# Halving the first expert selection of each layer, and moving every fourth row's dot product from VectorE to GpSimd and ScalarE

## The chip, the core and the metric

The program runs on one core of a Trainium2 chip. A core has TensorE (PE in the profile: matrix products), VectorE (DVE), ScalarE (ACT), GpSimd (POOL) and SyncE (SP, which here only issues transfers), each with an instruction queue of its own that it works through in order, and 16 DMA engines that move data between the chip's memory (HBM) and the on-chip buffer SBUF. Engines wait for each other through semaphores. The metric is the device time of one execution in microseconds (us); all arithmetic is in float32.

## The reference, cut to what matters

256 tokens of width 1024 pass through two layers (attention, then a feed-forward "PEER" block), and after them through a third block with recurrent mixers and a mixture of experts, which the change doesn't touch. The PEER block, for a chunk `xc` of 128 tokens:

```python
q = (xc @ wq).reshape(128, 8, 2, 128)                 # 8 heads, 2 sides
sc = jnp.einsum('chpd,hpnd->chpn', q, sub_keys)       # 128 key scores for each head and side
s1, i1 = lax.top_k(sc[:, :, 0], 16)
s2, i2 = lax.top_k(sc[:, :, 1], 16)
cand = s1[..., :, None] + s2[..., None, :]            # 256 candidates for each head
cidx = i1[..., :, None] * 128 + i2[..., None, :]
top_s, pos = lax.top_k(cand, 16)
eidx = take_along_axis(cidx, pos)                     # 16 of 16384 experts for each head
g = softmax(top_s)
a = gelu(einsum('chkd,cd->chk', u[eidx], xc))         # dot product with the expert's u
out = einsum('chk,chkd->cd', g * a, v[eidx])          # weighted sum of the experts' v
```

So each token picks 8 x 16 = 128 experts for each layer. For each the row `u` (1024 numbers) is multiplied with the token and summed up, and the row `v` is weighted and added.

## The kernel before, in words

Tokens lie on the 128 partitions. Each layer `l` has a **first chunk** (attention of tokens 0 to 127, then the peer queries and key scores), written out engine by engine, and a **peer stage** of 256 **rows**: row `n` is the n-th chosen expert of every token of a chunk (rows 0 to 127 of tokens 0 to 127, the others of tokens 128 to 255). In one row:

- GpSimd issues the gather (`gather`, line 2705): one indirect DMA brings to each partition the 2048 numbers (u and v) of its token's expert, 1 MB in all, into one of 8 landing places (`GATHERS = 8`; place `n % 8`). It waits until the numbers of the experts are there (`idx`), and for row n - 8 to have been used by TensorE.
- VectorE makes the dot product (`dots`, line 1551): one instruction that multiplies and sums, 128 x 1024, both inputs in SBUF, followed by a short one that reads out the accumulator.
- ScalarE (`weigh`, line 125) takes gelu of it, scales it by the softmax weight and writes a diagonal matrix of 64 columns.
- TensorE multiplies this with the row's v: 8 matmuls (`weighted_sum`, line 155; 64x64 tiles in the rows of the profile), and adds up in PSUM over 128 rows.

The experts are chosen by VectorE in **selections** (`route(q)`), four for a layer, each of four heads, for 64 rows (q = 0: rows 0 to 63). A selection is cut into 24 **pieces** (`yield`): 8 of `topk` over 128 scores, one that adds up candidates (128 x 1024), 4 of `topk` over 256 candidates, one of small steps, 6 over a one-hot table `OH` (128 x 1024: compare, multiply, reduce, for two sides), and the last steps with `idx_u`. `route(0)` runs whole before the first row. `route(q + 1)` has one piece on every second row of the 64 before (k = 2, 4, ... 48), `weights` (sum and reciprocal for the softmax) comes at k = 54, `exp_of` on ScalarE at k = 50.

Beside the rows each engine runs a **background**: rows 3, 5, ... 59 carry the attention of tokens 128 to 255 and their queries and key scores (`second_chunk`), later rows the third block's context (features in layer 0, states in layer 1) and in layer 0 the next layer's first projections. Each engine advances its background by one step at a fixed row (`beside`; GpSimd five rows later than its gathers count). So the order on each engine is written out by hand, and one engine's wait for another's background step holds back its rows as well. SyncE loads the weights (2 MB blocks) when their places in the `ring` come free.

In layer 0 the first chunk also has twelve `modulation` products with weights of their own, and the first gather waits until the tenth of them has left the place that it lands in (`("used", "w_mod", 10, 1)`). In layer 1 there is nothing of that; the gathers of places 2 to 7 wait for the queries' weights to be used.

## Time and profile before

| | us |
|---|---|
| median of three runs | 2847.54 |
| the runs | 2843.93 to 2849.05 |
| the profiled execution | 2847.81 |
| its span in the profile | 2846.0 |
| TensorE busy | 2144.6 (75%) |
| VectorE busy | 1585.1 (56%) |
| ScalarE busy | 832.7 (29%) |
| GpSimd busy | 749.6 (26%) |
| peer stage of layer 0, first gather to last sum | 191.4 to 948.4 |
| peer stage of layer 1 | 1096.6 to about 1825 |

How to read it: the busy shares are means over stages with different limits. Rows arrive fastest every 2.5 us in both peer stages, and the times at which a row is gathered, multiplied and summed can be followed in the trace one by one, since each row has one gather (line 2705), one dot product (line 1551), one 128x64 ScalarE instruction and 8 matmuls. The granted TensorE clock is a mean over a stretch, as a share of 2.4 GHz.

### The profile page before, as it was taken

Reading aid. Unit: us, or ns where it says so; the run is one execution under the profiler, and the core shown is the slowest. Engines: PE = TensorE matmul, PEld = TensorE weight load, DVE = VectorE, ACT = ScalarE, POOL = GpSimd, SP = SyncE. Lnnn points to the kernel's source line nnn. Section 1 sums busy time; section 2 is a strip of 40 time slices with the busy share of each in tenths; the row PEclk is TensorE's granted clock in tenths of the full one; section 3 lists DMA queues with packets and bytes.
Section 4 is the critical chain, followed back from the end, with each engine's and each line's share of the span. In section 5 each row is a group of like instructions: output and inputs, shape, how many; then the busy total and the mean of one; then the engine's idle time right before and its main releaser. Section 6 shows DMA issues by size and latency. Waiting matters only on the chain.

```text
span 2846.0 us, 33622 instructions
## 1 busy us (share of the span) xinstructions
PE 2144.6 (75%) x11828; PEld 1079.6 (38%) x11828; DVE 1585.1 (56%) x3312; ACT 832.7 (29%) x2340; POOL 749.6 (26%) x675
## 2 busy tenths in 40 slices
PE   6886767767567683776666667598987878988897
PEld 3552332222012262343332223276875443333332
DVE  5268648578446528856889877646555242222222
ACT  2215333433333312433343444323221111111111
POOL 1113434334335012334454445211111000000000
PEclk9888877778669786888998898899998889999999
DMA  7588999989999615899999899802111369999994
GB/s 274 213 339 314 408 422 405 422 339 393 422 421 412 239 67 212 327 422 406 416 396 397 329 421 415 359 33 88 58 45 63 119 281 415 420 420 419 417 419 186
DMA packets 122690, 894.55 MB, mean 314 GB/s; under 512 B 16400, under 2 KB 16912, under 8 KB 21776
## 3 DMA queue, kind: packets, MB, share of 16 engines
q0 software_dynamic: 77760, 545.30, 47.1%
q1 hardware_dynamic: 44752, 347.01, 30.1%
q8 instruction: 95, 1.56, 0.2%
q14 instruction: 83, 0.68, 0.1%
HBM read 893.82 MB, written 4.72 MB: 316 GB/s over the span
## 4 chain that ended last, share of the span: by engine, by line
PE 40%; DVE 27%; DMA 24%; ACT 4%; issue 3%; POOL 1%; SPq 0%; DVEq 0%; PEldq 0%; ACTq 0%; POOLq 0%
PE ps L155 39%; DMA ring<-in_peer_uv,idx_u 15%; DVE ring L1551 7%; DVE arena L76 5%; DMA ring<-in_w_gu 4%; ACT arena L125 3%; DMA arena<-in_peer_uv,idx_u 2%; DVE arena L1551 2%; DVE iu L113 2%; DVE arena L109 2%; PE ps L158 1%; DVE arena L97 1%; DVE small L93 1%; DMA arena<-in_w_gu 1%; DVE arena L118 1%
## 5 line engine op out<-in xcount | busy, mean ns | idle before, releaser
L155 PE MATMUL ps<-ring,arena 64*64 64x512 f32 (+3 forms) x4512 | 843.6, 715 | 339.4 <-ACT arena L125 293.0
L155 PE MATMUL ps<-arena 128*128 128x128 f32 (+8 forms) x3496 | 653.1, 501 | 196.8 <-ACT arena L125 160.3
L1551 DVE CUSTOM_DVE_ANT_0 ring<-ring,h 128x1024 f32<-128x1024 f32 x384 | 479.5, 1249 | 258.4 <-DMA ring<-in_peer_uv,idx_u 223.6
L2705 POOL DMA_INDIRECT ring<-in_peer_uv,idx_u x384 | 428.9, 1117 | 516.7 <-PE ps L155 477.3
L155 PEld LDWEIGHTS ps<-ring,arena 64*64 64x64 f32 (+3 forms) x4512 | 211.3, 149 | 841.3 <-ACT arena L125 578.1
L125 ACT ACTIVATE arena<-arena 128x1 f32<-128x1 f32 (+2 forms) x1051 | 270.8, 258 | 841.6 <-DVE arena L1551 739.7
L155 PEld LDWEIGHTS ps<-arena 128*128 128x128 f32 (+4 forms) x3496 | 323.3, 175 | 480.2 <-ACT arena L125 273.9
L125 ACT ACTIVATE arena<-ps 128x512 f32<-128x512 f32 (+2 forms) x222 | 122.7, 553 | 773.4 <-PE ps L155 702.5
L76 DVE TENSOR_TENSOR arena<-arena,ps 128x512 f32<-128x512 f32 (+1 forms) x154 | 90.9, 591 | 391.4 <-ACT arena L125 312.2
L155 PE MATMUL ps<-ring,hT 128*128 128x512 f32 (+2 forms) x832 | 281.2, 496 | 4.7 <-ACT hT L125 2.4
L2705 POOL DMA_INDIRECT arena<-in_peer_uv,idx_u x128 | 145.4, 1136 | 335.3 <-PE ps L155 259.5
L1551 DVE CUSTOM_DVE_ANT_0 arena<-arena,h 128x1024 f32<-128x1024 f32 x128 | 158.3, 1237 | 102.7 <-DMA arena<-in_peer_uv,idx_u 91.0
L125 ACT ACTIVATE arena<-cst,arena 128x64 f32<-128x64 f32 x512 | 178.1, 348 | 96.1 <-PE ps L155 50.7
L155 PEld LDWEIGHTS ps<-ring,hT 128*128 128x128 f32 x832 | 158.4, 198 | 116.4 <-issue 102.1
L134 POOL TENSOR_TENSOR small<-small,cst 128x1 f32<-128x1 f32 (+3 forms) x46 | 48.7, 1059 | 561.5 <-DVE small L84 561.5
L155 PE MATMUL ps<-hT,ring 128*128 128x128 f32 (+1 forms) x1280 | 185.0, 306 | 5.0 <-ACT hT L125 5.0
L155 PEld LDWEIGHTS ps<-hT,ring 128*128 128x128 f32 x1280 | 171.6, 199 | 29.8 <-issue 19.9
L97 DVE COPY arena<-ps 128x512 f32<-128x512 f32 (+3 forms) x116 | 70.4, 607 | 138.6 <-PE ps L155 72.9
L2829 POOL DMA_INDIRECT arena<-x_tab,iu x28 | 28.8, 1028 | 440.3 <-PE ps L158 342.5
L158 PE MATMUL ps<-cst,arena 128*128 128x128 f32 x602 | 98.5, 307 | 54.2 <-DVE arena L76 30.5
L158 PEld LDWEIGHTS ps<-cst,arena 128*128 128x128 f32 x602 | 77.0, 157 | 121.4 <-issue 46.0
L134 POOL TENSOR_TENSOR arena<-arena,cst 128x512 f32<-128x512 f32 (+2 forms) x48 | 52.8, 1100 | 207.4 <-DVE arena L76 110.2
(128 smaller groups left out, 1509.8 us busy)
## 6 DMA issues: line engine op xcount, KB each, us to landing
ring<-in_w_gu SPq DMA_DIRECT2D x98, 1024.0 KB, 22.5
ring<-in_w_down SPq DMA_DIRECT2D x52, 1024.0 KB, 22.6
ring<-in_peer_wq SPq DMA_DIRECT2D x16, 2048.0 KB, 11.3
arena<-in_w_gu SPq DMA_DIRECT2D x30, 1024.0 KB, 22.3
ring<-in_w_in SPq DMA_DIRECT2D x10, 2048.0 KB, 18.5
ring<-in_w_mod SPq DMA_DIRECT2D x16, 1024.0 KB, 7.3
arena<-in_w_in SPq DMA_DIRECT2D x6, 2048.0 KB, 11.8
ring<-in_w_o SPq DMA_DIRECT2D x6, 2048.0 KB, 8.2
```

What stands on the lines that cost most here:

```text
L76: self.done(self.e.tensor_tensor(o, a, b, op), *names)
L93: self.done(self.e.tensor_reduce(o, a, AX, op), *names)
L97: self.done(self.e.tensor_copy(o, a), *names)
L109: self.done(self.e.max(out=o, in_=a), *names)
L113: self.done(self.e.max_index(o, m, a), *names)
L125: self.done(self.e.activation(o, a, f, **k), *names)
L134: self.done(self.e.tensor_tensor(o, a, b, op), *names)
L155: return self.e.matmul(o, lhsT, rhs, start=start, stop=stop, skip_group_check=True)
L158: return self.e.transpose(o, src, ident)
L1551: v.done(v.e.tensor_tensor_reduce(out=row, in0=row, in1=h[:, n // 128, :], scale=1.0, scalar=0.0, op0=ALU.mult, op1=ALU.add, accum_out=aa[ ...
L2705: g.e.indirect_dma_start(out=landing(l, n), out_offset=None, in_=d["peer_uv"], in_offset=bass.IndirectOffsetOnAxis(ap=idx_u[:, n:n + 1], a ...
L2829: g.e.indirect_dma_start(out=m.xg[s % 4], out_offset=None, in_=x_tab, in_offset=index(m.row_of, s), bounds_check=T - 1, oob_is_err=False). ...
```

## The change

1. The first selection of each layer is made in two halves, of two heads each. `route`, `weights` and `exp_of` get the parameters `first` and `number`. `route(0, 0, 2)` runs whole before the first row; `route(0, 2, 2)` has one of its 15 pieces on each row from 0, and the rest at row 15 (`HALF_PIECES = 15`). The first half gives the indices of rows 0 to 31, the second those of rows 32 to 63.
2. To give the first half its scores early, TensorE makes the key scores of block 0 (two heads) after the first quarter of the second block of queries, and ScalarE takes them before it takes that block.
3. `route(1)` of each layer starts later and goes faster: one piece on each of the rows 17 to 40 in place of every second row from 2 to 48.
4. Rows 3, 7, 11, ... 255 (`DOTS_ASIDE`, 64 in a layer) have no dot product on VectorE. GpSimd multiplies the row with the tokens in place (`product`, `tensor_tensor` 128 x 1024, just after it has issued the gather of 6 rows later, `ASIDE_AT = 6`), and ScalarE sums up with a copy that accumulates (128 x 1024) ahead of its gelu.

```diff
@@ TensorE, first_chunk
-                for i in range(2):
-                    run(queries(l, i, 0, free))
-                key_scores(l, 0, 0, free)
+                run(queries(l, 0, 0, free))
+                q = queries(l, 1, 0, free)
+                next(q)
+                key_scores(l, 0, (0,), free)
+                run(q)
+                key_scores(l, 0, (1,), free)
@@ VectorE, peer
-                for _ in route(0):
+                for _ in route(0, 0, 2):
                     pass
+                second_half = route(0, 2, 2)
                 first = finish(0)
                 for n in range(256):
-                    dots(n)
+                    if n not in DOTS_ASIDE:
+                        dots(n)
                     if n == 1:
-                        weights(0)
+                        weights(0, 0, 2)
+                    if n < HALF_PIECES:
+                        next(second_half, None)
+                    if n == HALF_PIECES:
+                        for _ in second_half:
+                            pass
+                    if n == HALF_PIECES + 5:
+                        weights(0, 2, 2)
                     q, k = n // 64, n % 64
                     if q < 3:
                         if k == 1:
                             pieces = route(q + 1)
-                        if k in range(2, 2 + 2 * ROUTE_PIECES, 2):
+                        if k in (range(2, 2 + 2 * ROUTE_PIECES, 2) if q else range(HALF_PIECES + 2, HALF_PIECES + 2 + ROUTE_PIECES)):
                             next(pieces, None)
@@ ScalarE, weigh
-                    a.wait_ge(*at("dots", l, n))
+                    if n in DOTS_ASIDE:
+                        row = landing(l, n)[:, 0:D]
+                        a.wait_ge(*at("product", l, n))
+                        a.act(row, row, ACT.Copy, accum_out=w)
+                    else:
+                        a.wait_ge(*at("dots", l, n))
                     a.act(w, w, ACT.Gelu)
@@ GpSimd, peer
+                def product(n):
+
+                    row = landing(l, n)[:, 0:D]
+                    g.wait_ge(*at("landed", l, n))
+                    g.tt(row, row, h[:, n // 128, :], ALU.mult, ("product", l, n))
+
-                for n in range(256 + 5):
+                for n in range(256 + ASIDE_AT):
                     if n < 256:
                         gather(n)
+                    if n - ASIDE_AT in DOTS_ASIDE:
+                        product(n - ASIDE_AT)
```

On TensorE, in the first chunk of either layer (`hT,ring` are the queries of heads pair by pair, 32 to a block; `arena` 128x128 the key scores):

```order
-L155 MATMUL ps<-hT,ring 128x128 x64
-L155 MATMUL ps<-arena 128x128 x8
+L155 MATMUL ps<-hT,ring 128x128 x40
+L155 MATMUL ps<-arena 128x128 x4
+L155 MATMUL ps<-hT,ring 128x128 x24
+L155 MATMUL ps<-arena 128x128 x4
```

The first four key scores stand ahead of 24 query products, where all eight stood behind all of them.

On VectorE, rows 9 to 13 of layer 0's peer stage in the changed kernel (`ISA` with `h` is a dot product, `ISA 128x1` its read-out; 128x512 and 128x32 are the second half's one-hot steps; COPY and `small<-ps` are background):

```order
L1561 ISA ring,arena<-ring,h 128x1024
L1561 ISA arena 128x1
L93 TENSOR_REDUCE arena<-arena 128x32
L76 TENSOR_TENSOR arena<-cst,arena 128x512
L1561 ISA ring,arena<-ring,h 128x1024
L1561 ISA arena 128x1
L76 TENSOR_TENSOR arena<-arena 128x512
L1561 ISA ring,arena<-ring,h 128x1024
L1561 ISA arena 128x1
L93 TENSOR_REDUCE arena<-arena 128x32
```

Rows 10, 12 and 13 have their dot product here with a piece of the second half behind each; row 11 has its piece and no dot product. Before, all of these rows had one, and every second of them a `topk` piece of `route(1)`.

On GpSimd, from the first gather of layer 0 on, before:

```order
L2705 DMA arena<-in_peer_uv,idx_u 128x2048 x2
L2705 DMA ring<-in_peer_uv,idx_u 128x2048 x6
L2705 DMA arena<-in_peer_uv,idx_u 128x2048 x2
L2705 DMA ring<-in_peer_uv,idx_u 128x2048 x6
L2705 DMA arena<-in_peer_uv,idx_u 128x2048 x2
```

and in the changed kernel:

```order
L2731 DMA arena<-in_peer_uv,idx_u 128x2048 x2
L2731 DMA ring<-in_peer_uv,idx_u 128x2048 x6
L2731 DMA arena<-in_peer_uv,idx_u 128x2048 x2
L134 TENSOR_TENSOR ring<-ring,h 128x1024
L2731 DMA ring<-in_peer_uv,idx_u 128x2048 x4
L134 TENSOR_TENSOR ring<-ring,h 128x1024
L2731 DMA ring<-in_peer_uv,idx_u 128x2048 x2
```

A product now stands behind the gather of row 9, 13, 17 and so on, ahead of the next gather.

## Rows read from the trace of the kernel before

**Rows 1.** The page's first line.

```profile
span 2846.0 us, 33622 instructions
```

**Rows 2.** Timeline (start us, us, instruction, idle before), layer 1's start: GpSimd's first gather, VectorE's first selection.

```profile
1096.57 1.04 POOL L2705 DMA_INDIRECT arena<-in_peer_uv,idx_u  x1 [59.36 <-DVE idx_u L97]
...
1062.20 0.29 DVE L109 MAX8 arena<-arena 128x8 f32<-128x128 f32 x1 [22.34 <-ACT arena L125]
```

**Rows 3.** Timeline, layer 0's start: GpSimd's first gather; VectorE's indices, second dot product.

```profile
191.36 1.17 POOL L2705 DMA_INDIRECT arena<-in_peer_uv,idx_u  x1 [67.13 <-PE ps L155]
...
182.25 0.20 DVE L97 CAST idx_u<-arena 128x64 uint32<-128x64 f32 x1
...
200.33 1.23 DVE L1551 CUSTOM_DVE_ANT_0 arena<-arena,h 128x1024 f32<-128x1024 f32 x1 [1.64 <-DMA arena<-in_peer_uv,idx_u]
```

**Rows 4.** Busy time by stretch: engine busy (instructions); PE clock, DMA share, GB/s last.

```profile
203.50:314.50 111.00, 76.78 (x420) 27.63 (x416) 97.11 (x229) 50.92 (x155) 39.62 (x35) 0.82 0.87 345
580.00:660.00 80.00, 47.06 (x244) 16.55 (x243) 66.93 (x156) 26.86 (x80) 32.09 (x27) 0.70 0.88 348
740.00:840.00 100.00, 67.45 (x316) 11.16 (x320) 48.79 (x82) 36.29 (x122) 38.64 (x39) 0.65 1.01 421
...
1340.00:1420.00 80.00, 57.20 (x388) 27.88 (x384) 71.45 (x159) 28.96 (x96) 42.38 (x36) 0.89 1.00 407
...
1580.00:1660.00 80.00, 56.64 (x369) 24.93 (x365) 61.77 (x94) 35.79 (x108) 42.30 (x36) 0.85 0.88 356
```

**Rows 5.** Waits of VectorE from 203.5 to 314.5 (total, times, longest), the DMA's.

```profile
DVE ring L1551 <- DMA ring<-in_peer_uv,idx_u: 1.2, 1, 1.2
```

**Rows 6.** Timeline of layer 1's queries and key scores: ScalarE's copies, TensorE's key scores.

```profile
1052.53 0.60 ACT L125 ACTIVATE arena<-ps 128x512 f32<-128x512 f32 x1 [10.01 <-PE ps L155]
...
1059.47 2.01 PE L155 MATMUL ps<-arena 128*128 128x128 f32 x16
...
1061.52 0.60 ACT L125 ACTIVATE arena<-ps 128x512 f32<-128x512 f32 x1 [0.35 <-PE ps L155]
```

**Rows 7.** Timeline of VectorE in layer 1's first selection: where its parts begin.

```profile
1075.87 0.23 DVE L97 CAST arena<-iu 128x128 f32<-128x128 uint32 x1
...
1086.88 0.20 DVE L82 TENSOR_SCALAR iu<-iu 128x64 uint32<-128x64 uint32 x1
...
1088.06 1.23 DVE L76 TENSOR_TENSOR arena<-cst,arena 128x1024 f32<-128x1024 f32 x1
...
1095.61 0.22 DVE L89 SCALAR_TENSOR_TENSOR arena<-arena 128x64 f32<-128x64 f32 x1
```

**Rows 8.** All VectorE instructions of one shape (busy, mean ns); then two dot products in sequence.

```profile
L76 DVE TENSOR_TENSOR arena<-cst,arena 128x512 f32<-128x512 f32 x26 | 18.0, 692 | 1.5 <-PE ps L155 0.6
...
273.68 1.22 DVE L1551 CUSTOM_DVE_ANT_0 ring<-ring,h 128x1024 f32<-128x1024 f32 x1
...
275.05 1.23 DVE L1551 CUSTOM_DVE_ANT_0 ring<-ring,h 128x1024 f32<-128x1024 f32 x1
```

**Rows 9.** GpSimd's 256-wide products as a group, then GpSimd's and VectorE's timeline near 1597.

```profile
L134 POOL TENSOR_TENSOR arena<-arena 128x256 f32<-128x256 f32 x4 | 3.0, 751 | 6.0 <-DVE arena L76 6.0
...
1596.89 1.26 POOL L134 TENSOR_TENSOR ring<-arena,cst 128x512 f32<-128x512 f32 x1 [5.53 <-DVE arena L76]
1598.23 2.13 POOL L134 TENSOR_TENSOR arena<-arena,cst 128x512 f32<-128x512 f32 x1
...
1596.95 2.28 DVE L1551 CUSTOM_DVE_ANT_0 ring<-ring,h 128x1024 f32<-128x1024 f32 x1
```

**Rows 10.** Timeline of GpSimd in layer 0's opening: a background step between two gathers.

```profile
282.42 1.67 POOL L134 TENSOR_TENSOR small<-small,cst 128x8 f32<-128x8 f32 x1 [4.33 <-DVE small L84]
```

**Rows 11.** GpSimd's gathers from 1340 to 1420 as a group (busy, mean ns, idle before).

```profile
L2705 POOL DMA_INDIRECT ring<-in_peer_uv,idx_u x24 | 26.6, 1110 | 26.7 <-PE ps L155 23.6 <-issue 2.9
```

**Rows 12.** Timeline of ScalarE: an accumulating 128x1024 pass and its read-out.

```profile
952.90 1.06 ACT L125 ACTIVATE arena<-h 128x1024 f32<-128x1024 f32 x1 [6.50 <-DVE h L82]
953.87 0.19 ACT L125 ACTIVATION_READ_ACCUMULATOR arena<-h 128x1 f32 x1
```

More of the change, by code:

```diff
@@ L221 @@
 MOD_ASIDE = (4, 6, 8, 10)
+DOTS_ASIDE, ASIDE_AT = range(3, 256, 4), 6
 def padded(n, *gens):
@@ L638, in queries, with key_scores @@
                 pe.done(t, ("ps", "q", l, i, c), ("used", "wq", l, i, c))
-            def key_scores(l, c, hf, among=range(8)):
+            def key_scores(l, c, js, among=range(8)):
                 pe.wait_ge(*at("loaded", "keys", l))
-                for j in (2 * hf, 2 * hf + 1):
+                for j in js:
                     b = fresh("s", l, c, j, among=among)
@@ L712, in first_chunk @@
                 modulation(6)
-                key_scores(l, 0, 1, free)
+                key_scores(l, 0, (2, 3), free)
                 modulation(7)
@@ L1503, in peer, with route @@
                 s = 2 * l + 1
-                def route(q):
+                def route(q, first=0, number=4):
                     c, hf = UNITS[q]
                     sc = SC[:, 1024 * hf:1024 * hf + 1024]
-                    for j in (2 * hf, 2 * hf + 1):
+                    part = slice(256 * first, 256 * (first + number))
+                    for j in (2 * hf + first // 2, 2 * hf + (first + number - 1) // 2):
                         v.wait_ge(*at("out", "s", l, c, j))
-                    yield from topk(8, P, vv, ii, sc, SC2)
-                    v.cp(iif, ii)
-                    v4 = vv.rearrange("p (h s k) -> p h s k", h=4, s=2)
-                    i4 = iif.rearrange("p (h s k) -> p h s k", h=4, s=2)
-                    cand = sc.rearrange("p (h a b) -> p h a b", h=4, a=16)
+                    sc, other = sc[:, part], SC2[:, part]
+                    k1, k2 = (slice(w * first, w * (first + number)) for w in (32, 16))
+                    yield from topk(2 * number, P, vv[:, k1], ii[:, k1], sc, other)
+                    v.cp(iif[:, k1], ii[:, k1])
+                    v4 = vv[:, k1].rearrange("p (h s k) -> p h s k", h=number, s=2)
+                    i4 = iif[:, k1].rearrange("p (h s k) -> p h s k", h=number, s=2)
+                    cand = sc.rearrange("p (h a b) -> p h a b", h=number, a=16)
@@ L1516, in route @@
                     v.tt(cand, bc(v4[:, :, 0, :], 3, 16), bc(v4[:, :, 1, :], 2, 16), ALU.add)
                     yield
-                    yield from topk(4, 256, tv, pos, sc, SC2)
-                    v.ts(pu, pos, 4, None, ALU.logical_shift_right, None)
-                    v.cp(f1, pu)
-                    v.ts(pu, pos, 15, None, ALU.bitwise_and, None)
-                    v.cp(f2, pu)
-                    g, t3 = gs[:, 64 * q:64 * q + 64], heads(tv, 4)
-                    v.tt(heads(g, 4), t3, t3[:, :, 0:1].to_broadcast([P, 4, 16]), ALU.subtract, ("g", l, q))
+                    yield from topk(number, 256, tv[:, k2], pos[:, k2], sc, other)
@@ new lines, in route @@
+                    v.ts(pu[:, k2], pos[:, k2], 4, None, ALU.logical_shift_right, None)
+                    v.cp(f1[:, k2], pu[:, k2])
+                    v.ts(pu[:, k2], pos[:, k2], 15, None, ALU.bitwise_and, None)
+                    v.cp(f2[:, k2], pu[:, k2])
+                    to = slice(64 * q + 16 * first, 64 * q + 16 * (first + number))
+                    t3 = heads(tv[:, k2], number)
+                    v.tt(heads(gs[:, to], number), t3, t3[:, :, 0:1].to_broadcast([P, number, 16]), ALU.subtract,
+                         ("g", l, q, first))
@@ L2337, in peer, with exp_of @@
             def peer(l, background):
-                def exp_of(q):
-                    g = gs[:, 64 * q:64 * q + 64]
-                    a.wait_ge(*at("g", l, q))
-                    a.act(g, g, ACT.Exp, ("exp g", l, q))
+                def exp_of(q, first=0, number=4):
+                    g = gs[:, 64 * q + 16 * first:64 * q + 16 * (first + number)]
+                    a.wait_ge(*at("g", l, q, first))
+                    a.act(g, g, ACT.Exp, ("exp g", l, q, first))
                 def weigh(n):
                     w = aa[:, n:n + 1]
-                    a.wait_ge(*at("dots", l, n))
+                    if n in DOTS_ASIDE:
[4 more added lines that the diff above has]
+                        a.wait_ge(*at("dots", l, n))
                     a.act(w, w, ACT.Gelu)
-                    a.wait_ge(*at("weights", l, n // 64))
+                    a.wait_ge(*at("weights", l, n // 64, 2 if 32 <= n < 64 else 0))
                     a.act(w, w, ACT.Copy, scale=gs[:, n:n + 1])
@@ L2353, in weigh @@
                     a.act(diagonals[n % 2], C("ident2"), ACT.Copy, ("diagonal", l, n), scale=w)
-                exp_of(0)
+                exp_of(0, 0, 2)
                 for n in range(256):
                     weigh(n)
+                    if n == HALF_PIECES + 1:
+                        exp_of(0, 2, 2)
                     if n == NORM_AT[1]:
```

47 lines of the change are left out of this document (24 added, 23 removed).

## The prediction, as it was put on record

> **What bounds the kernel now.** I read the stretches of busy time first, then the waits of each engine inside them, then the timeline, row by row. In a peer stage the rows land 2.5 us apart at best: the stretch from 740 to 840 moves 421 GB/s at a DMA share of 1.01, and there VectorE is busy for 48.8 of 100 us and GpSimd for 38.6 [rows 4]. So a faster VectorE or an earlier gather gives nothing there. Where the GB/s are below 421 the DMA engines starve, and that is the time that can be had. There are three kinds. (a) The opening of each stage: 203.5 to 314.5 has 345 GB/s with VectorE busy for 97.1 of 111 us [rows 4], and it waited 1.2 us for a landing in all of it [rows 5]; the rest of its idle time is mostly gaps of some tens of ns between instructions. VectorE is the bound for about 35 rows, and the loss is 111 x (1 - 345/421) = 20 us. Layer 1 repeats it. (b) Middles: 580 to 660 (348 GB/s, VectorE 66.9 of 80, loss 14 us) and, in layer 1, 1340 to 1420 (407, VectorE 71.5 of 80, loss 3 us) to 1580 to 1660 (356, loss 12 us) [rows 4]. (c) Before the first gather of layer 1 GpSimd sat idle for 59.4 us until VectorE had the indices, and of that the selection was running from 1062.20 [rows 2]. In layer 0 it is not so: VectorE had its indices at 182.45 and the gather began at 191.36, released by TensorE, which had to free the place of a modulation weight [rows 3].
>
> **Part 1, the first selection in halves.** Its steps [rows 2, 7]: 8 topk of 128 from 1062.20 to 1075.87, 13.7 us; cast, sum and 4 topk of 256 to 1086.88, 11.0 us, of which the sum and cast take 1.5; small steps 1.2; six one-hot passes from 1088.06 to 1095.61, 7.55 us; the last three 0.7. In all 34.1 us. A half has 4 topk (6.8), a sum of 512 (0.69 in place of 1.23, with the cast 0.9), 2 topk of 256 (4.7), small steps (1.0, they are mostly fixed cost), six passes of 512 at 0.692 and a gap [rows 8] (4.3), and 0.6: 18.4 us. The two halves cost 36.8, 2.7 more than the whole. It also starts earlier: ScalarE has the first queries at 1053.1, a quarter of the second block of queries (6.9 us between [rows 6]'s first two) is 1.7 us, half the key scores 1.0, ScalarE's copy 0.7. That is 1056.0, 6.2 us ahead of 1062.20. So the first gather of layer 1 comes 34.1 - 18.4 + 6.2 = **21.9 us earlier**. Other waits allow it: the queries' weights that hold places 2 to 7 are used up at about 1075, and those gathers would be issued from 1077 on. In layer 0 the gather is held by the modulation weight [rows 3], which the change does not hasten: **0**. VectorE just idles longer, since its next instruction is the dot product of row 0 and the second half stands behind it.
>
> **What it costs in the opening.** 18.4 us of selection now lie inside the stretch that VectorE bounds. What counts is VectorE's time when it comes to row 23: about there GpSimd, which waits for a background result of VectorE until 282.42 [rows 10], issues the gather after which the DMA queue stayed full. Up to row 23: second half +18.4; two `weights` for one +0.6; `route(1)` has 6 pieces of 1.7 (10.2) where it had 8 of 1.7, the sum of 1.5 and two of 2.4 (19.9): -9.7; five dot products (3, 7, 11, 15, 19) that are gone, 1.37 us each from start to start [rows 8]: -6.9; idle time ahead of rows 1 and 2 that a piece now fills (1.64 us [rows 3] and as much again ahead of row 2): -2.8. Sum -0.4 us. From 23 to 41 pieces come on each row, some 9 us more than before, less four dot products; but before, VectorE waited for landings from row 35 on so the DMA set the pace, and I take this as covered; if the cover is gone it costs up to 6 us in each layer.
>
> **Part 2, dot products aside.** Its price has no direct row: no 128x1024 product on GpSimd. 256 wide takes 0.75, 512 wide 1.26 [rows 9], which gives 2.3 by the slope, 2.5 by doubling; I take 2.35. ScalarE adds 1.06 and a read-out of 0.19, overlapping, together 1.2 [rows 12]; it has the time (50.9 of 111 us busy [rows 4]). The second `exp_of` brings two table loads to ScalarE in each layer, hidden for the same reason. On VectorE 64 x 1.37 = 88 us for each layer go away; it is worth something only in (a) and (b).
>
> Against it stands what happens at 1596.9. A 512-wide product begins on GpSimd at 1596.89 and takes 1.26; a dot product begins on VectorE at 1596.95 and takes 2.28, where it takes 1.23 elsewhere [rows 8, 9]: +1.05, nearly all of what was left of the product. The next GpSimd product takes 2.13 where 1.26 is normal: it stood behind the dot product. So a dot product and a product exclude each other. The Trainium skill has the rule for this ("SBUF — State Buffer", "Who interferes with whom"): a VectorE instruction with two inputs in SBUF and a GpSimd instruction that reads SBUF share a read port, and the second fully blocks. The trace agrees.
>
> What a product of 2.35 us costs VectorE depends on what stands behind the dot product after which it gets the port: a topk piece (1.7 or 2.4, one input) leaves 0 to 0.7 us of stall, a one-hot pass or another dot product up to 2.35. By that: products of rows 3, 7, 11, 15, 19: 0, 0.3, 1.5, 1.7, 0.7 = **+4.2 in the opening of each layer**, 0.8 each; bounds 0 and 5 x 2.35 = 12. So an opening costs -0.4 + 4.2 = **+4**.
>
> Middle of layer 0 (rows 128 to 172): 11 dot products, -15; stalls of 1.2 each, since every second row has a piece, +13: **-2**. Middle of layer 1 (rows 68 to 172): 26 of them, -36, stalls +31 to +34. But GpSimd has its own budget there: from 1340 to 1420, 32 gathers of 1.11 to 1.15 [rows 11] and 0.3 between, some 46 us; 8 products at 2.35 and a wait for the port of about 0.6, 25 us; 4 background products of 512 at some 1.6, 7 us with gaps. (The stretch has 42.4 busy without the products and the gaps [rows 4].) 78 of 80 us: it is nearly full, and in order. I put **+1** for this middle: -3 from VectorE, +4 from GpSimd.
>
> In the steady stretches GpSimd has 40 gathers (49 us with gaps) and 10 products (27 us) for 100 us, and a row's detour is about 2.5 us, while a landing place has a round of 8 x 2.5 = 20 us, of which dot product, diagonal and sum take some 5: 0. At each layer's end, row 255 is one of those aside: after its landing 2.35 + 0.1 + 1.2 in place of 1.23, and nobody hides it: **+2.5 for each layer**.
>
> **Sum.** Layer 0: 0 + 4 - 2 + 2.5 = +4.5. Layer 1: -21.9 + 4 + 1 + 2.5 = -14.4. Together -9.9 us. The profiled execution had 2847.8 around a span of 2846.0 [rows 1]; the median is 2847.5. So 2837.8 by the one and **2837.6** by the other.
>
> **The rivals.** *Relief in full*: products slip between VectorE's one-input instructions, stalls near zero. Then the openings cost -0.4 each (-9 against my sum), layer 0's middle gets back most of 14 us (-10), layer 1's middle some 15 of its 25 to 30 us (-16): 2803. For it: topk makes up most of the pieces. Against it: 1596.95. Chance 0.12. *GpSimd becomes the bound (slower)*: place, rows 62 to 252 of layer 1 and the VectorE-heavy parts of layer 0. It decides when a gather with its gap costs over 1.5 us and a product with its port wait over 3.5: 4 x 1.5 + 3.5 + 0.9 of background = 10.4 us for four rows against 9.9 of DMA time. Over 47 groups of four in layer 1 that is +24, in layer 0 about +8 for the part with much VectorE work: 2838 + 32 - 4 (already counted) = 2866. For it: gathers already stretch from 0.95 to 1.1 and more beside dot products [rows 11]. Against it: where VectorE is slower, the gathers are asked for later. Chance 0.17. *The opening takes back the head start*: stalls at their upper bound (+8 in each layer) and the pieces of rows 24 to 41 uncovered (+6 each, of which I believe half): 2838 + 16 + 6 = 2860 at the worst, typically +10: 2848, no change. For it: VectorE is busy throughout; layer 0 pays and has no head start. Chance 0.18. *The change does not hasten layer 1*: a wait for queries' weights or key scores holds the first gather; 2838 + 15 = 2853. Chance 0.03.
>
> **How the numbers follow.** Forecast 0.50, between 2826 and 2843 by itself. A measurement of this kernel can tell some 0.2%, 5.7 us, from no change, so faster means under 2841.8. Forecast: faster 0.43, same 0.06, slower 0.01. Relief: faster 0.12. GpSimd: same 0.02, slower 0.15. Opening: faster 0.03, same 0.10, slower 0.05. No hastening: same 0.01, slower 0.02. Sums: faster 0.58, same 0.19, slower 0.23. The range runs from 2812, which takes in a good part of the relief, to 2862, which takes in the opening and the smaller half of GpSimd's case.
>
> **What would show it.** Right: first gather of layer 1 about 22 us earlier after the end of layer 0's stage, 32 us after the start of its peer queries in place of 54; layer 0's first gather at about 191 still; landing of row 41 in layer 0 about 4 us later against the first gather; GpSimd products of 2.3 to 3.5 us, dot products of 1.23 and of up to 3.5; no change of 2.5 us for each row in the steady stretches; 2.5 us more from the last landing to the last sum. Wrong: dot products that show no stretching; GpSimd busy for over 90% with gathers that start at once after the instruction ahead, and DMA share under 0.95 in layer 1 beyond row 62; a lower TensorE clock with waits on it.

## The result, and the profile after

The changed kernel takes 3100.61 us (median of four runs, 3097.31 to 3108.66), the kernel before, beside it on the same chip, 2848.30 (2843.93 to 2851.71). The ratio is 1.0887, with a 95% interval from 1.0872 to 1.0901: **slower by 252 us**, where 2837.6 was forecast and 2862 was the upper end of the range. The profiled execution took 3102.16 us.

The page of the kernel after: its span, the busy times, what the DMA engines moved in 40 slices, and the chain that ended last.

```profile
span 3100.3 us, 33798 instructions
...
PE 2219.8 (72%) x11828; PEld 1138.2 (37%) x11828; DVE 1575.8 (51%) x3094; ACT 985.2 (32%) x2602; POOL 1089.2 (35%) x803
...
GB/s 283 210 350 241 386 383 325 327 319 347 388 396 332 250 82 246 266 384 359 325 321 311 307 307 340 313 301 65 93 58 55 58 102 416 418 420 419 418 418 204
...
PE 46%; POOL 17%; ACT 11%; DVE 11%; DMA 8%; issue 6%; SPq 0%; PEldq 0%; ACTq 0%; DVEq 0%; POOLq 0%
```

The chain of the kernel before, beside it:

```profile
PE 40%; DVE 27%; DMA 24%; ACT 4%; issue 3%; POOL 1%; SPq 0%; DVEq 0%; PEldq 0%; ACTq 0%; POOLq 0%
```

The span is 254 us longer than before [rows 1]. No engine is near full: TensorE and VectorE have smaller shares than before, ScalarE (29 to 32%) and GpSimd (26 to 35%) larger ones, since they have the new work. VectorE did 128 dot products less and is busy for nearly as long (1575.8 us), so what is left on it got longer. In the chain GpSimd now has 17% in place of 1, and the DMA engines 8% in place of 24. In the peer stages (the 4th to 13th and 17th to 27th slice of 77.5 us) the values are 241 to 396 GB/s; none reaches the 421 that the kernel before had from 740 to 840 [rows 4].

The same view as [rows 4], of after: opening and late stretch of layer 0, middle and late stretch of layer 1.

```profile
203.50:314.50 111.00, 67.81 (x344) 27.19 (x344) 91.53 (x235) 55.32 (x152) 49.33 (x36) 0.73 0.73 280
...
900.00:1000.00 100.00, 57.38 (x288) 17.05 (x284) 45.97 (x60) 36.82 (x113) 61.28 (x45) 0.77 0.93 354
...
1450.00:1530.00 80.00, 47.01 (x272) 19.58 (x262) 63.95 (x143) 30.69 (x90) 52.72 (x35) 0.74 0.85 320
...
1900.00:2000.00 100.00, 60.53 (x348) 27.16 (x349) 61.30 (x81) 42.46 (x122) 62.35 (x43) 0.73 0.88 326
```

From 900 to 1000 VectorE is busy for 46 of 100 us, GpSimd for 61, ScalarE for 37, and the rows still come at 354 GB/s. Nobody is full, so the engines wait for each other in turn. Who waits for whom is in the waits of the whole span (total, times, longest):

```profile
ACT ring L125 <- POOL ring L134: 596.9, 121, 11.6
POOL ring L2731 <- PE ps L155: 465.8, 200, 11.3
...
POOL arena L2731 <- PE ps L155: 244.6, 89, 65.3
```

ScalarE waits 4.9 us on average for each of 121 products (L134) before it can sum one up; this wait is new. GpSimd's gathers (L2731) wait for TensorE's sums, and that is no more than in the kernel before:

```profile
POOL ring L2705 <- PE ps L155: 477.3, 255, 13.7
```

But there only further gathers and a few background steps stood behind a gather that waits; now products do. The groups of instructions:

```profile
L1561 DVE CUSTOM_DVE_ANT_0 ring<-ring,h 128x1024 f32<-128x1024 f32 x256 | 383.1, 1496 | 228.5 <-DMA ring<-in_peer_uv,idx_u 202.4
...
L134 POOL TENSOR_TENSOR ring<-ring,h 128x1024 f32<-128x1024 f32 x128 | 310.2, 2423 | 13.3 <-DMA ring<-in_peer_uv,idx_u 10.8
```

A product takes 2.42 us, and a dot product 1.50 where it was 1.23 [rows 8]. GpSimd reaches its products late: it stood idle before them for 13 us in all, so nearly every row had landed before GpSimd came to it.

Last, one round in a stretch of layer 0 whose rows land 2.5 us apart at this point: GpSimd, then ScalarE, then TensorE.

```profile
869.29 0.93 POOL L2731 DMA_INDIRECT ring<-in_peer_uv,idx_u  x1 [0.30 <-issue]
870.24 2.62 POOL L134 TENSOR_TENSOR ring<-ring,h 128x1024 f32<-128x1024 f32 x1
873.02 1.78 POOL L2731 DMA_INDIRECT ring<-in_peer_uv,idx_u  x1 [0.15 <-issue]
877.38 1.57 POOL L2731 DMA_INDIRECT ring<-in_peer_uv,idx_u  x1 [2.59 <-PE ps L155]
879.26 0.94 POOL L2731 DMA_INDIRECT arena<-in_peer_uv,idx_u  x1 [0.30 <-issue]
880.50 0.94 POOL L2731 DMA_INDIRECT arena<-in_peer_uv,idx_u  x1 [0.31 <-issue]
881.47 2.35 POOL L134 TENSOR_TENSOR ring<-ring,h 128x1024 f32<-128x1024 f32 x1
...
872.90 1.06 ACT L125 ACTIVATE ring<-ring 128x1024 f32<-128x1024 f32 x1 [5.13 <-POOL ring L134]
...
874.70 0.35 ACT L125 ACTIVATE arena<-cst,arena 128x64 f32<-128x64 f32 x1
...
875.10 1.98 PE L155 MATMUL ps<-ring,arena 64*64 64x512 f32 x8 [5.45 <-ACT arena L125]
```

**The circle.** By counting gathers, the two products are those of rows 191 and 195, and the gathers between them bring rows 198 to 201. Row 191's product ends at 872.86. ScalarE has waited 5.13 us for it, sums it up and writes the diagonal by 875.05; TensorE, idle for 5.45 us, adds the row's v until 877.08; that frees the landing place that the gather of row 199 has been waiting for, and it goes out at 877.38. Behind it in GpSimd's queue stand the gathers of rows 200 and 201, and only behind those the product of row 195, which starts at 881.47. Row 195 had landed at 874.4, 7 us earlier. ScalarE, in order, can't do rows 196 to 198 before it, though VectorE has the dot products of rows 196 and 197 by 880.6. So product m waits for gather m + 4, that for the sum of row m - 4, and that for product m - 4. Four rows cost 11.2 us from product to product (2.6 product, 2.2 ScalarE, 2.0 TensorE, 0.3, 4.1 for three gathers), where the DMA engines need 4 x 2.48 = 9.9. Before, GpSimd had no part in a row beyond its gather, and a gather that waited held back the use of no row that had landed.

### The profile page after: what moved, and what is told of

It reads as the page before. It is cut to its first block, busy times and chain, and to the rows that moved or that the text cites. A ratio compares the mean times of both kernels' runs of the same rounds, so it can differ in the third digit from the quotient of the medians.

```text
span 3100.3 us, 33798 instructions
## 1 busy us (share of the span) xinstructions
PE 2219.8 (72%) x11828; PEld 1138.2 (37%) x11828; DVE 1575.8 (51%) x3094; ACT 985.2 (32%) x2602; POOL 1089.2 (35%) x803
## 4 chain that ended last, share of the span: by engine, by line
PE 46%; POOL 17%; ACT 11%; DVE 11%; DMA 8%; issue 6%; SPq 0%; PEldq 0%; ACTq 0%; DVEq 0%; POOLq 0%
PE ps L155 45%; POOL ring L134 8%; ACT arena L125 5%; ACT ring L125 4%; POOL ring L2731 4%; DMA ring<-in_w_gu 3%; POOL arena L2731 3%; DVE arena L76 3%; PE ps L158 2%; ACT L125 1%; DVE ring L1561 1%; DMA ring<-in_peer_uv,idx_u 1%; DVE arena L97 1%; DMA arena<-in_w_gu 1%; DVE arena L89 1%
## 5 line engine op out<-in xcount | busy, mean ns | idle before, releaser
L155 PE MATMUL ps<-ring,arena 64*64 64x512 f32 (+3 forms) x4512 | 883.5, 758 | 636.7 <-ACT arena L125 591.5
L155 PE MATMUL ps<-arena 128*128 128x128 f32 (+8 forms) x3496 | 681.0, 529 | 88.7 <-ACT arena L125 59.6
L2731 POOL DMA_INDIRECT ring<-in_peer_uv,idx_u x384 | 467.5, 1218 | 508.2 <-PE ps L155 465.8
L155 PEld LDWEIGHTS ps<-ring,arena 64*64 64x64 f32 (+3 forms) x4512 | 229.5, 160 | 1115.5 <-ACT arena L125 815.5
L1561 DVE CUSTOM_DVE_ANT_0 ring<-ring,h 128x1024 f32<-128x1024 f32 x256 | 383.1, 1496 | 228.5 <-DMA ring<-in_peer_uv,idx_u 202.4
L155 PEld LDWEIGHTS ps<-arena 128*128 128x128 f32 (+4 forms) x3496 | 348.0, 188 | 395.9 <-issue 192.9
L125 ACT ACTIVATE arena<-arena 128x1 f32<-128x1 f32 (+1 forms) x1053 | 271.1, 257 | 258.7 <-DVE arena L1561 154.5
L125 ACT ACTIVATE ring<-ring 128x1024 f32<-128x1024 f32 (+1 forms) x136 | 141.2, 1038 | 598.0 <-POOL ring L134 596.9
L134 POOL TENSOR_TENSOR ring<-ring,h 128x1024 f32<-128x1024 f32 x128 | 310.2, 2423 | 13.3 <-DMA ring<-in_peer_uv,idx_u 10.8
L1561 DVE CUSTOM_DVE_ANT_0 arena<-arena,h 128x1024 f32<-128x1024 f32 x128 | 197.7, 1545 | 146.1 <-DMA arena<-in_peer_uv,idx_u 132.7
L2731 POOL DMA_INDIRECT arena<-in_peer_uv,idx_u x128 | 137.3, 1073 | 293.3 <-PE ps L155 244.6
L134 POOL TENSOR_TENSOR small<-small,cst 128x1 f32<-128x1 f32 (+3 forms) x46 | 48.7, 1058 | 519.4 <-DVE small L84 519.4
L158 PE MATMUL ps<-cst,arena 128*128 128x128 f32 x602 | 103.3, 318 | 52.7 <-DVE arena L76 29.6
## 6 DMA issues: line engine op xcount, KB each, us to landing
ring<-in_w_gu SPq DMA_DIRECT2D x98, 1024.0 KB, 21.9
```

The costliest lines, as they stand in the source:

```text
L125: self.done(self.e.activation(o, a, f, **k), *names)
L134: self.done(self.e.tensor_tensor(o, a, b, op), *names)
L155: return self.e.matmul(o, lhsT, rhs, start=start, stop=stop, skip_group_check=True)
L158: return self.e.transpose(o, src, ident)
L1561: v.done(v.e.tensor_tensor_reduce(out=row, in0=row, in1=h[:, n // 128, :], scale=1.0, scalar=0.0, op0=ALU.mult, op1=ALU.add, accum_out=aa[ ...
L2731: g.e.indirect_dma_start(out=landing(l, n), out_offset=None, in_=d["peer_uv"], in_offset=bass.IndirectOffsetOnAxis(ap=idx_u[:, n:n + 1], a ...
```

## The experiments

**Which part loses.** Two kernels, one part each. The first has the halves and every dot product on VectorE:

```diff
-DOTS_ASIDE, ASIDE_AT = range(3, 256, 4), 6
+DOTS_ASIDE, ASIDE_AT = range(0), 6
```

> The first selection in halves alone; every row's dot product stays on VectorE. My working of part 1 gave -21.9 us for layer 1's earlier gather and about -0.4 us plus nothing for stalls in each opening, so 2826 us, first gather of layer 1 22 us earlier against the end of layer 0's stage. A rival says that the second half, inside a stretch that VectorE bounds, and route(1) at one piece on each row cost more than that: 2848 to 2870 us. Either way the 252 us of the whole change should not be here.

Measured: 2848.25 us against 2847.04, ratio 1.0008 [0.9998, 1.0017]: no change, so the rival's 2848 and not the 2826 expected. Layer 1's first gather, and two stretches of busy time of this kernel (layer 0's opening, layer 1's):

```profile
1083.34 1.04 POOL L2731 DMA_INDIRECT arena<-in_peer_uv,idx_u  x1 [37.41 <-DVE idx_u L97]
```

```profile
203.50:334.50 131.00, 84.29 (x432) 29.50 (x432) 118.56 (x295) 55.92 (x166) 41.40 (x37) 0.77 0.83 328
1087.00:1200.00 113.00, 69.46 (x359) 26.84 (x358) 98.74 (x264) 50.82 (x145) 39.64 (x35) 0.74 0.82 318
```

GpSimd waits 37.4 us where it waited 59.4 [rows 2], and the time from layer 0's last landing to this gather fell from 152.5 to 128.5. The head start of 24 us is there. It is given back: from its first gather on, row 47 lands after 170.1 us in layer 0 (before: 161.9) and 169.2 in layer 1 (161.1), and the whole stages are 11.8 and 11.4 us longer. VectorE is busy for 118.6 of 131 us there, at 328 GB/s. Two openings of 8 us and a little more behind them eat 24.

The second kernel is the kernel before with part 2 alone (the `product` function and the split of `weigh`, nothing of the halves).

> Every fourth row's dot product on GpSimd and ScalarE alone, the selection whole. If part 2 is the cause of the loss, 3100 to 3130 us (the change's 3100 plus the head start of some 20 us that is not there). If only both together lose (a crowded opening), under 2950 us.

Measured: 3106.02 us, 1.0923 [1.0905, 1.0941]; ScalarE's wait for products is the same as after:

```profile
ACT ring L125 <- POOL ring L134: 599.5, 121, 12.3
```

So the whole loss belongs to part 2.

**The port or the circle.** Two causes stood: dot products and products exclude each other, or the product's place in GpSimd's queue. First the place: the product directly behind the gather of row m + 4, its background steps where they were.

```diff
-DOTS_ASIDE, ASIDE_AT = range(3, 256, 4), 6
+DOTS_ASIDE, ASIDE_AT = range(3, 256, 4), 4
-                for n in range(256 + ASIDE_AT):
+                for n in range(256 + 6):
```

> The whole change, but a product stands behind the gather of 4 rows later, not 6. Loop theory: behind the gather of row m+6, which waits for row m-2 to be summed, the product closes a circle gather 1.3 + product 2.4 + ScalarE 2.2 + TensorE 2.4 + two more rows 2.5 = 10.8 us for four rows, above the DMA's 9.9, and no transfer can hide it. With 4 it waits for row m-4, four rows a turn of about 8.3 us: 2850 to 2930 us. Port theory (VectorE and GpSimd shut each other out): the same products, the same dot products, 3080 to 3120 us.

Measured: 2893.10 us, 1.0172 [1.0139, 1.0205]. That gives back 0.0715 of the ratio, 204 us of 252 (some 10 either way). Waits and groups of this kernel:

```profile
POOL ring L2731 <- PE ps L155: 214.9, 121, 12.0
ACT ring L125 <- POOL ring L134: 184.4, 77, 8.6
```

```profile
L1561 DVE CUSTOM_DVE_ANT_0 ring<-ring,h 128x1024 f32<-128x1024 f32 x256 | 353.7, 1382 | 226.8 <-DMA ring<-in_peer_uv,idx_u 200.9 <-issue 2.5 <-DVE ring L97 0.5
L134 POOL TENSOR_TENSOR ring<-ring,h 128x1024 f32<-128x1024 f32 x128 | 312.0, 2437 | 139.1 <-DMA ring<-in_peer_uv,idx_u 137.3 <-issue 0.2
```

The products are as many and as long. What changed is the last column: GpSimd now waits 137 us for landings before its products, so it comes to them ahead of the data, and ScalarE's wait fell from 597 to 184 us.

Then the port: the product at its old place, replaced by three memsets of the same length that read nothing. The dot products of these rows are left out of the computation; every wait, the landing place and ScalarE's pass stay.

```diff
-                    g.tt(row, row, h[:, n // 128, :], ALU.mult, ("product", l, n))
+                    for k in range(2):
+                        g.wait_ge(g.sem, g.n)
+                        g.done(g.e.memset(row, 0.0))
+                    g.wait_ge(g.sem, g.n)
+                    g.done(g.e.memset(row[:, 0:512], 0.0), ("product", l, n))
```

> The whole change, but in place of the product GpSimd fills the row's u part with zeros three times (two of 1024, one of 512), which reads nothing from SBUF; the dot products of these rows are left out of the result. About 2.3 to 2.8 us for each row, as long as the product. Port theory: dot products on VectorE back to 1.23 us each, 2830 to 2900 us. Loop theory: dot products at 1.23 too, but still 3030 to 3110 us, since the circle is as long as before.

Measured: 3089.45 us, 1.0862 [1.0837, 1.0887].

```profile
L1561 DVE CUSTOM_DVE_ANT_0 ring<-ring,h 128x1024 f32<-128x1024 f32 x256 | 322.5, 1260 | 254.1 <-DMA ring<-in_peer_uv,idx_u 227.6 <-issue 1.3 <-DVE ring L97 0.5
...
L2743 POOL MEMSET ring<- 128x1024 f32 x256 | 245.6, 960 | 17.1 <-DMA ring<-in_peer_uv,idx_u 9.7
```

```profile
ACT ring L125 <- POOL ring L2745: 614.4, 121, 11.6
```

The dot products are back at 1.26 us, and the kernel is as slow as ever, with the same wait of ScalarE. Exclusion at the port is real, but as long as the circle sets the pace it costs nearly nothing: 0.0025 of the ratio, 7 us, some 8 either way.

**The size of the circle.** Two more points on its length: a product and a sum of 512 columns at the old place (half of the dot product left out), and the whole product behind gather m + 5.

```diff
-                    row = landing(l, n)[:, 0:D]
+                    row = landing(l, n)[:, 0:512]
-                    g.tt(row, row, h[:, n // 128, :], ALU.mult, ("product", l, n))
+                    g.tt(row, row, h[:, n // 128, 0:512], ALU.mult, ("product", l, n))
```

> The whole change (product behind the gather of 6 rows later), but GpSimd's product and ScalarE's sum take 512 of the 1024 columns; the other half of these dot products is left out of the result. It shortens one turn of the circle by 1.1 (GpSimd) + 0.4 (ScalarE) = 1.5 us for four rows, 128 turns. Loop theory: 192 us less where the circle is the bound all the time, so 2910 to 2960 us. If it were GpSimd's own busy time, the saving would be about 1.1 us a turn or less, 2960 us and over; if the mutual stalls of the port, write_only has shown that they are small: 3060 us and over.

```diff
-DOTS_ASIDE, ASIDE_AT = range(3, 256, 4), 6
+DOTS_ASIDE, ASIDE_AT = range(3, 256, 4), 5
-                for n in range(256 + ASIDE_AT):
+                for n in range(256 + 6):
```

> The whole change with a product behind the gather of 5 rows later. Loop theory: it waits for row m-3; a turn of four rows is that of the change less one row's share on ScalarE and TensorE (some 1.3 us), 9.5 us against the DMA's 9.9: nearly covered, 2900 to 2990 us, between the 2893 of four and the 3101 of six and nearer to four. A cause that does not depend on what stands ahead of the product would give the mean of both or no order at all.

Measured: 2905.49 us, 1.0201 [1.018, 1.0223], for the half product (its time fell a little below the range expected), and 2907.50, 1.0208 [1.0188, 1.0229], behind m + 5. ScalarE's waits, of the one and of the other:

```profile
ACT ring L125 <- POOL ring L134: 421.5, 119, 11.8
```

```profile
ACT ring L125 <- POOL ring L134: 305.9, 103, 6.5
```

The circle's length can be worked out from its parts in the fence of after, and stands against the pace that was measured in a piece of layer 0 with little background (rows 208 to 223, from landing to landing):

| kernel | circle worked out, us for four rows | us per row measured |
|---|---|---|
| before | none | 2.48 |
| after (m + 6) | 11.2 | 2.89 |
| memsets (m + 6) | 11.3 (they take 2.5 in place of 2.4) | 2.88 |
| product behind m + 5 | 10.0 (one gather of 1.24 less) | 2.52 |
| half product (m + 6) | 9.6 (-1.1 product, -0.5 sum) | 2.52 |
| product behind m + 4 | 8.7 (two gathers less) | 2.50 |

Above 9.9 the circle is the pace, under or at it the DMA engines are. (Four rows at 2.89 are 11.6, a little over the 11.2; from row 192 to row 224 the mean is 2.79, which gives 11.2.) With background steps in a row each engine's part grows, and there the circles of 9.6 and 10.0 should bind too: that ScalarE still waits 421.5 and 305.9 us for products in these two kernels speaks for this being where they lose their 2%, but no run separates it from the port's share.

**The port without the circle.** The memsets behind gather m + 4 (the two edits together; the same part of the computation is left out).

> As product_after_4 (2893 us), with three GpSimd fills that read nothing in place of the product; the dot products of these rows are left out of the result. What is left of the port's price once the circle is off the path: dot products had 353.7 + 193.6 = 547 us for 384 rows, 1.42 each, and should fall to 1.24. If the port costs what I forecast (0.8 to 1.2 us for each product in the stretches that VectorE bounds, some 55 products), 2830 to 2855 us. If it costs nothing, 2885 to 2900.

Measured: 2846.32 us, 0.9989 [0.9977, 1.0]; against the real product at the same place (1.0172) it is 0.0183 less, 52 us, some 10 either way.

```profile
PE 2152.8 (76%) x11828; PEld 1098.7 (39%) x11828; DVE 1443.2 (51%) x3094; ACT 984.9 (35%) x2602; POOL 1069.4 (38%) x1059
```

VectorE is busy for 1443.2 us where it was 1550.5 with the real product: 107 us of stretching for 128 products, and half of it reaches the time. The dot products have 65 us of it (547.3 against 482.1 us in all); the rest is on other VectorE instructions, 22 us on element-wise ones of two inputs (TENSOR_TENSOR of 128x512 and 128x1024), and some on one-input ones: six 128x128 casts take 1.24 us each in place of 0.27. So of 252 us some 204 are the circle and some 50 the port, if the circle is taken away first. The other way round the port gives back 7 us (the memsets at m + 6 against after) and the circle then 249 (the memsets at m + 4 against those at m + 6, 0.0873 of the ratio): most of the port's price shows only when the circle is gone. The rest, what halves and removed dot products bring with both out of the way, is -3 us, not more: that kernel still has ScalarE waiting 188 us for its memsets.

**Fewer products.** One row in eight, at the old place, should have had a circle of twice the time to close in.

```diff
-DOTS_ASIDE, ASIDE_AT = range(3, 256, 4), 6
+DOTS_ASIDE, ASIDE_AT = range(7, 256, 8), 6
```

> The whole change with only rows 7, 15, ... 255 aside (32 in a layer), product behind the gather of 6 rows later. Loop theory: the circle closes once in 8 rows, 10.8 us plus four rows more at the pace of ScalarE and TensorE (some 1.3 each) = 16 us against 19.8 of DMA time, so it is covered, and half of the port's 47 us is left: 2865 to 2890 us. If each product simply cost its 2 us (252 us for 128 products), 2848 + 126 = 2974 us.

Measured: 2933.07 us, 1.0295 [1.0274, 1.0315]. The expectation of 2865 to 2890 failed. Two stretches of busy time of layer 0:

```profile
800.00:900.00 100.00, 60.55 (x320) 12.52 (x320) 44.63 (x73) 40.54 (x133) 57.10 (x45) 0.71 1.01 421
900.00:1000.00 100.00, 68.46 (x358) 21.20 (x354) 53.16 (x88) 38.32 (x122) 58.13 (x44) 0.86 0.89 363
```

The steady rows run at 421 GB/s, as worked out. The loss lies where the rows carry background: openings, middles, the last 32 rows. The reading, before the next run: ScalarE works in order, so while it waits for a late product its background step waits too, and with it the steps of TensorE and VectorE that want its result, and the gather that wants TensorE. If so, half the products lose much less at m + 4; if it were the number of products, nothing would change.

```diff
-DOTS_ASIDE, ASIDE_AT = range(3, 256, 4), 6
+DOTS_ASIDE, ASIDE_AT = range(7, 256, 8), 4
-                for n in range(256 + ASIDE_AT):
+                for n in range(256 + 6):
```

> As one_row_in_8 (2933 us), with the product behind the gather of 4 rows later. In that run the rows from 176 to 239 of layer 0, which have no background, stood at 2.49 us, as the circle theory says, and the loss lay in the rows with background: there a turn of the circle is longer by the background that stands on ScalarE, TensorE and GpSimd in between. If that is so, taking the circle away at the same number of products brings it to 2848 plus half of the port's 47, 2860 to 2880 us. If the loss comes from the products as such (GpSimd's time, the port), it stays at 2915 to 2935.

Measured: 2874.83 us, 1.0108 [1.0089, 1.0126], 0.0187 of the ratio less from the place alone, 53 us, some 8 either way; ScalarE's wait fell to

```profile
ACT ring L125 <- POOL ring L134: 113.3, 44, 8.8
```

from 252.7 at m + 6. The place decides here as well. Which engine's background closes the circle in which stretch was not taken apart.

**What is left of the idea.** All dot products on VectorE, layer 0's first selection made in full ahead of the first row (there is nothing to gain there [rows 3]), the halves in layer 1 alone, three pieces of its second half in the wait for the first landing, and `route(1)` of layer 1 spread so that fewer of its pieces come before row 23.

```diff
+                for _ in range(3 if l else 15):
+                    next(second_half, None)
+                if l:
+                    spots = (*range(13, 23, 2), *range(24, 43))
+                else:
+                    spots = range(2, 2 + 2 * ROUTE_PIECES, 2)
...
-                    if n < HALF_PIECES:
+                    if n < 12 * l:
...
-                        if k in (range(2, 2 + 2 * ROUTE_PIECES, 2) if q else range(HALF_PIECES + 2, HALF_PIECES + 2 + ROUTE_PIECES)):
+                        if k in (range(2, 2 + 2 * ROUTE_PIECES, 2) if q else spots):
```

> All dot products on VectorE. Layer 0: both halves before the first row (its gather is held by a modulation weight anyway), route(1) as before. Layer 1: halves, with three pieces of the second half ahead of the first dot product, one on each of rows 0 to 11, and route(1) from row 13 on, every second row to 21 and each from 24 to 42. Theory: halves_only lost in layer 0's opening 11.8 us that nothing pays for, and the same in layer 1 against a head start of 24. So layer 0 goes back to 753 us, and layer 1 keeps the head start and loses 5 to 9 in its opening: 2829 to 2835 us. Rival: the opening takes back whatever the gather gains, since VectorE has the same work: 2845 to 2850.

Measured: 2836.56 us against 2847.66, 0.9957 [0.994, 0.9973]: 12 us faster than the kernel before, and just above the 2829 to 2835 expected.

```profile
1075.41 1.04 POOL L2737 DMA_INDIRECT arena<-in_peer_uv,idx_u  x1 [37.42 <-DVE idx_u L97]
```

The first gather comes 21.2 us ahead of its time before [rows 2], and row 47 lands 164.1 us after it, 3 us later than before and not 8; the stage as a whole gives back 9. Whether what happens up to row 23 decides that or VectorE's load beyond it was the last question: the same kernel with all of `route(1)` behind row 23 (`spots = range(24, 48)`).

> As halves_in_layer_1 (2836.6 us), but in layer 1 route(1) has its 24 pieces on rows 24 to 47 and none on rows 13 to 21. If VectorE's time at about row 23 sets the opening and what follows is covered by the DMA, as I forecast, five pieces of 1.7 us less ahead of row 23 save up to 8 us: 2828 to 2833. If VectorE bounds the rows beyond 23 too (a piece on each row and the attention of the second chunk), as halves_only's lag of 10 to 17 us on rows 24 to 40 suggests, the same work only comes later: 2834 to 2842.

Measured: 2839.96 us, 0.9967 [0.9955, 0.998]. Row 23 lands 1.6 us earlier than in the kernel just above (74.2 us after the first gather against 75.8), row 47 0.7 us earlier, and the time is no better. The step of row 23 alone does not decide; the load on VectorE counts over the whole opening.

## Why the prediction was wrong, point by point

- **The step that failed** is the sentence "In the steady stretches ... a row's detour is about 2.5 us, while a landing place has a round of 8 x 2.5 = 20 us ...: 0". It looks at the detour as a latency with slack around it. But the product has a place in a queue, and the queue ahead of it holds gathers that wait for rows before it. The terms of the circle were at hand (product 2.35, ScalarE 1.2 and its usual steps, dot product, diagonal and sum some 5, gathers 0.95 to 1.1; the rule for row n - 8 and the product behind the gather of row 9 stand in the description of the kernels); they were never put in a line from product to product. The runs show in place of the 0 a circle of 11.2 us for four rows against the DMA engines' 9.9. Price: 204 us of the 252 (the product behind m + 4 against after).
- **"GpSimd becomes the bound"** (0.17, 2866) named the right engine for the wrong reason, its fill. The 78 of 80 us worked out, gaps included, were for rows at 407 GB/s. In the middle of layer 1 (1450 to 1530) the changed kernel is at 320 GB/s with GpSimd busy for 52.7 of 80 us, and 24 us of its idle time there are gathers' waits for TensorE's sums. The product behind m + 4 shows that fill is not what costs: with the same instructions, GpSimd is busy for 60.8 us between 1450 and 1530 and the rows come at 393 GB/s, 204 us less in all. GpSimd is late because it waits, not because it is full, and a count of busy microseconds can't show that.
- **The port.** The mechanism is as forecast: with a product about, dot products take up to 4.05 us (the one that starts at 925.20, 0.61 ahead of a product), the products 2.35 alone and 2.42 on average. Its stalls were put at 4.2 us for each opening and 13 and 31 to 34 of VectorE's time for the middles, 52 to 55 in all. Measured once the circle is out of the way: 107 us of VectorE's time over everything, part of it on one-input instructions, which had been counted as free, and 52, some 10 either way, in the result. In the openings (row 47, real product against memset, both behind m + 4) it was 9.0 and 5.4 us, above the 4.2 taken and inside the bounds of 0 and 12.

  The Trainium skill ("SBUF — State Buffer", "Who interferes with whom") lets a VectorE instruction with two inputs in SBUF and a GpSimd instruction that reads SBUF block each other, and leaves out a GpSimd instruction that only writes it. The runs agree on both sides of it: dot products take 1.50 us on average in the kernel with products, 1.26 in the one with memsets that read nothing.
- **The head start**: 21.9 forecast (its terms, 1053.1 + 1.7 + 1.0 + 0.7, give 1056.5 and not 1056.0, so 21.4 as written); 24.0 measured with the halves alone, 20.4 in the changed kernel (152.5 to 132.1 us). Row 255's own detour, which makes layer 0's last sum later, is 1.6 of the 3.6 between them; the other 2.0 lie between that sum and the gather and were not looked into. Its layer 0 term, 0, is right as well: the first gather is at 190.30, held by TensorE as before.
- **The opening**: -0.4 without the port was forecast, with five dot products gone (6.9) in it (twice 1.64 of idle time would be 3.3 there, not 2.8). Without them +6.5 follows from the same sum, and the halves alone show 7.1 at row 23 in layer 0 (81.1 us against 74.0 from the first gather) and 6.5 in layer 1: that sum was sound. In the changed kernel row 23 is at 81.1 and 82.7, so on balance with what the products cost, the dot products that are gone bought nothing there. What I "took as covered", the pieces of rows 24 to 41, was not quite: about 1 us more to row 47 in layer 0, 1.6 in layer 1, and 3 to 4 over the rest of the stage.
- **The relief of VectorE**, 15 and 36 us of its time in the two middles before stalls, and the ground of the rival of 2803, did not come. The memset kernel behind m + 4 has it with no port to pay and stands at -3 us. ScalarE's wait of 188 us for the memsets is what stands there in its place; that this takes all of the gain was not shown by a run of its own.
- **The tails**, +2.5 each: last landing to last sum is 5.8 and 11.4 us, where it was 4.3 in both layers. That is +1.5 and +7; why the second is so long was not looked into.

## What to carry to other kernels

Before compute is put on an engine that also issues transfers, write down what stands ahead of it in that queue and what each of those waits for, and follow it until it comes back to the same kind of instruction: if it does, the length of that circle against the pace of the transfers is the price, however empty the engines are. Put such work ahead of the waits that depend on it; moving a product by two gathers was worth 204 us here. And of an earlier start count what it pushes into the stretch behind it: half to all of 24 us went that way.

## What the runs showed of the hardware that was not expected

- A 128x1024 product of two float32 inputs takes GpSimd 2.35 us alone, a memset of the same size 0.96. The memsets left VectorE's dot products alone.
- A gather that starts while a dot product runs is held up by it. VectorE beside the gathers in the fence of after:

```profile
871.93 2.02 DVE L1561 CUSTOM_DVE_ANT_0 ring<-ring,h 128x1024 f32<-128x1024 f32 x1 [1.25 <-DMA ring<-in_peer_uv,idx_u]
...
876.91 1.23 DVE L1561 CUSTOM_DVE_ANT_0 ring<-ring,h 128x1024 f32<-128x1024 f32 x1 [2.96 <-DMA ring<-in_peer_uv,idx_u]
...
879.41 1.23 DVE L1561 CUSTOM_DVE_ANT_0 ring<-ring,h 128x1024 f32<-128x1024 f32 x1 [1.26 <-DMA ring<-in_peer_uv,idx_u]
...
881.86 3.04 DVE L1561 CUSTOM_DVE_ANT_0 ring<-ring,h 128x1024 f32<-128x1024 f32 x1 [1.22 <-DMA ring<-in_peer_uv,idx_u]
```

  The dot product of 881.86 starts 0.39 us into a product and takes 1.81 us longer than alone; what was left of the product is 1.96. The gather at 873.02 starts while a dot product has 0.93 to run, and takes 1.78, 0.84 more than its usual 0.94; the one at 877.38 starts with 0.76 to run and takes 1.57, 0.63 more. The one at 879.26 starts ahead of a dot product and takes 0.94. They put 0.6 us of such waiting into the circle. No run was made for the gathers, but the trace of the kernel before has enough of them: of 126 that start with over 0.3 us of a dot product to run, 117 take over 1.1 us (median 1.58); of 338 that start with no VectorE instruction so far from its end, 7 do (median 0.95). Beside element-wise instructions of two inputs (TENSOR_TENSOR) the gathers split in two: 14 of 16 take over 1.1 us (median 1.28) where VectorE reads both inputs from SBUF, none of 12 (0.94) where one comes from PSUM.
- In the circle TensorE's sum stands at the lower clock. Two stretches of busy time of after: one over the eight matmuls of row 191, before which TensorE had been idle for 5.45 us, and one over the eight of row 194, behind the sums of two other rows; then the timeline of the latter.

```profile
874.00:877.00 3.00, 1.90 (x12) 0.64 (x16) 0.09 (x1) 2.23 (x9) 0.80 (x1) 0.50 1.01 421
...
879.40:880.60 1.20, 1.09 (x12) 0.14 (x4) 1.19 (x2) 0.00 (x0) 0.89 (x2) 1.00 0.99 369
```

```profile
879.46 1.03 PE L155 MATMUL ps<-ring,arena 64*64 64x512 f32 x8
```

At a granted 0.50, the level of 1.2 GHz, a row's sum takes 1.98 us; at 1.00, 2.4 GHz, 1.03. The circle of 11.2 us holds one at the lower level, 0.95 us longer than at the other; the whole circle is 1.3 us over the DMA's pace. Over the whole span the same 11828 matmuls kept TensorE busy for 2219.8 us, 75 more than before.
